# The last 16 rows of five 2 MB loads sent as 8-row transfers, and an encoder's first matmul units reordered around its filter layer

## The reference, cut to what matters

```
xn = rms_norm(x, norm1_w)
q, k, v, r, a_low, hy_in, gates = split(xn @ w_in)            # w_in: 1024 x 8224
o_gla = gla_branch(q, k, v, r, a_low, ...)
h1   = sin(freq * (z @ hy_ffn_w1 + b1))                        # z: 256 x 33, the filter's features
h2   = sin(freq * (h1 @ hy_ffn_w2 + b2));  taps = (h2 @ hy_ffn_w3) * decay
o_hy = hyena_branch(hy_in, ..., taps)
h = x + (sigmoid(g_gla) * (o_gla @ w_branch_gla) + sigmoid(g_hy) * (o_hy @ w_branch_hy)) @ w_out
out = 0
for e in range(32):                                            # 12 MB of weights for each expert
    out += combine[:, e] * (swiglu(hn @ w_gate_up[e] + b) @ w_down[e] + b)
return rms_norm(h + out, norm_f_w)
```

## Time and profile before

| | |
|---|---|
| median of 3 runs | 1237.72 us (1237.39 to 1237.72) |
| the profiled execution's own time | 1237.29 us |
| its span | 1235.4 us |
| PE busy | 1160.8 us, 94% |
| HBM read | 453.29 MB, 368 GB/s over the span |
| granted TensorE clock | 0.999 |

### The profile page before, as it was taken

One profiled execution on the slowest core, in us unless ns is written; L12 is line 12 of the kernel. 1 busy time (PEld: TensorE's weight loads), 2 busy tenths in 40 slices (PEclk: granted clock), 3 DMA queues, 4 the chain that ended last, 5 costly groups with the idle time before them and its releaser, 6 DMA issues.

```text
span 1235.4 us, 13704 instructions
## 1 busy us (share of the span) xinstructions
PE 1160.8 (94%) x5828; PEld 599.6 (49%) x5828; DVE 420.2 (34%) x703; ACT 266.9 (22%) x422; POOL 0.2 (0%) x4
## 2 busy tenths in 40 slices
PE   7999999999999999999999889888988898889987
PEld 6899968888533443443343324333433333333332
DVE  6777878756421221222112112111221121111112
ACT  6866546344210000010010001000100010000002
POOL 0000000000000000000000000000000000000000
PEclk9999999999999999999999999999999999999999
DMA  9454425698999999999999999999999999999996
GB/s 322 147 157 151 148 91 171 217 399 340 365 425 428 427 428 428 427 429 425 429 426 429 428 428 428 427 428 428 427 428 425 429 427 429 427 429 427 427 426 263
DMA packets 67292, 455.25 MB, mean 368 GB/s; under 512 B 6970, under 2 KB 23771, under 8 KB 39966
## 3 DMA queue, kind: packets, MB, share of 16 engines
q1 hardware_dynamic: 65654, 454.06, 89.8%
q10 hardware_dynamic: 1576, 0.29, 0.1%
HBM read 453.29 MB, written 1.05 MB: 368 GB/s over the span
## 4 chain that ended last, share of the span: by engine, by line
PE 64%; DMA 32%; DVE 2%; issue 1%; ACT 1%; DVEq 0%; ACTq 0%
DMA ring<-in_w_gate_up 28%; PE bank L1201 18%; PE bank L1219 12%; PE total L902 6%; PE bank L902 5%; PE total L890 4%; PE bank L890 4%; DMA ring<-in_w_down 3%; PE bank L960 2%; PE bank L1187 2%; PE bank L979 1%; PE total L1233 1%; PE total L1201 1%; PE bank L1208 1%; PE total L950 1%
## 5 line engine op out<-in xcount | busy, mean ns | idle before, releaser
L1201 PE MATMUL bank<-ring,hy_area 128*64 128x512 f32 x1984 | 444.6, 595 | 43.2 <-DMA ring<-in_w_gate_up 43.2
L1201 PEld LDWEIGHTS bank<-ring,hy_area 128*64 128x64 f32 x1984 | 136.8, 137 | 331.4 <-issue 244.6
L1219 PE MATMUL bank<-ring,xn_area 128*64 128x512 f32 x992 | 220.1, 595 | 0.3 <-DMA ring<-in_w_down 0.3
L2119 DVE TENSOR_SCALAR qk_area<-bank 128x512 f32<-128x512 f32 x31 | 21.4, 692 | 361.3 <-PE bank L1201 361.3
L1219 PEld LDWEIGHTS bank<-ring,xn_area 128*64 128x64 f32 x992 | 68.4, 137 | 134.6 <-issue 122.8
L1682 ACT ACTIVATE qk_area<-qk_area 128x512 f32<-128x512 f32 x32 | 20.2, 630 | 456.7 <-DVE qk_area L2119 456.7
L2130 DVE SCALAR_TENSOR_TENSOR xn_area_r<-bank,tmp_area,xn_area_r 128x512 fp32r<-128x512 f32 x31 | 23.3, 751 | 200.5 <-ACT xn_area_r L1693 200.5
L1823 DVE TENSOR_TENSOR front_r<-ring,slot_r 128x1024 fp32r<-128x1024 f32 x60 | 73.1, 1222 | 22.2 <-ACT slot_r L1493 22.2
L1493 ACT CAST slot_r<-ring 128x1024 fp32r<-128x1024 f32 x60 | 62.8, 1049 | 43.5 <-PE bank L902 23.2
L1693 ACT ACTIVATE xn_area_r<-bank,tmp_area 128x512 fp32r<-128x512 f32 x31 | 21.3, 687 | 234.9 <-PE bank L1219 221.0
L979 PE MATMUL bank<-tmp_area_r 128*128 128x512 f32 x124 | 38.0, 426 | 12.8 <-issue 8.6
(11 more groups left out here) (397 smaller groups left out, 1253.2 us busy)
## 6 DMA issues: line engine op xcount, KB each, us to landing
ring<-in_w_gate_up SPq DMA_DIRECT2D x116, 2048.0 KB, 37.0
ring<-in_w_down SPq DMA_DIRECT2D x54, 2048.0 KB, 38.9
ring<-in_w_in SPq DMA_DIRECT2D x31, 1024.0 KB, 5.7
ring<-in_w_gate_up SPq DMA_DIRECT2D x22, 1024.0 KB, 9.4
ring<-in_w_down SPq DMA_DIRECT2D x19, 1024.0 KB, 9.9
ring<-in_w_branch_gla SPq DMA_DIRECT2D x4, 1024.0 KB, 5.2
ring<-in_w_branch_hy SPq DMA_DIRECT2D x4, 1024.0 KB, 7.7
ring<-in_w_out SPq DMA_DIRECT2D x4, 1024.0 KB, 6.3
```

The costliest lines, as they stand in the source:

```text
L1201: last = pe.matmul(to[bk][half * CAP:(half + 1) * CAP, :], xeT[:, j, q, :], where(j, c), start=False, stop=(j == GU_CH - 1), skip_group_ch ...
L1219: last = pe.matmul(banks[to][half * CAP:(half + 1) * CAP, :], half_of(turned, f), where(j, c * D + half * 512), start=(f == 0), stop=(f == ...
L2119: nc.vector.tensor_scalar(gate, made[0][:, :], LIMIT, None, ALU.min).then_inc(gate_ready, 1)
```

## The change

It has two parts.

**In the expert stream**, five of the 170 loads of 2 MB are cut by rows: the first 112 rows in one transfer, and the last 16 in two transfers of 8 rows. They are the 9th of the 2 MB loads and every 34th after it. All other loads stay.

**At the start**, the filter's first matmul moves ahead of the transposes of x (stage `filter_in`), with its wait for `filt_loaded`; DVE's share of the filter layer stays where it was. The function for the first unit becomes `early_unit` and does the first three v units pass by pass; within the first pass it waits for each half of an `xT` tile apart, and ACT signals each half. Chunk 1 is loaded in halves as chunk 0 is, and the rest of `tab` and the small load `w_a` are issued after chunk 1.

```
+EVEN_ROWS = 112
+FEW_ROWS = 8
+SPLIT = tuple(n for n, width in LOADS if width == 2)[8::34]
+
+def row_parts(n):
+    if n not in SPLIT:
+        return [(0, P)]
+    return [(0, EVEN_ROWS)] + [(r, r + FEW_ROWS) for r in range(EVEN_ROWS, P, FEW_ROWS)]
...
-        count[s] += 16
+        count[s] += 16 * len(row_parts(n))
...
-    st = [("xT", n) for n in range(4)] + v0[:1] + [("wa_parts",), ("filter", 1)] + v0[1:] + ...
+    st = [("filter_in",)] + [("xT", n) for n in range(4)] + v0[:1] + [("wa_parts",), ("filter", 1)] + v0[1:] + ...
...
-                if c == 0:
+                if c < 2:
                     for i in range(UNITS_PER_CHUNK):
-                        sp.dma_start(unit_of(i), src[:, 2 * i:2 * i + 2, :]).then_inc([first_loaded, front_loaded[0]][i], 16)
+                        sp.dma_start(unit_of(2 * c + i), src[:, 2 * i:2 * i + 2, :]).then_inc([first_loaded[c], front_loaded[c]][i], 16)
...
-                sp.dma_start(ring[:, s * SLOT:(s + width) * SLOT], rows_of(*CHUNK_ORDER[n], width)).then_inc(moe_loaded[s], 16)
+                src = rows_of(*CHUNK_ORDER[n], width)
+                for r, to in row_parts(n):
+                    sp.dma_start(ring[r:to, s * SLOT:(s + width) * SLOT], src[r:to, :]).then_inc(moe_loaded[s], 16)
...
-            def first_unit():
+            def early_unit(u):
                 a_hi, a_lo = parts_of["xn"]
-                hi, lo = unit_hi(0), unit_of(0, as_r["front"])
-                pe.wait_ge(w_hi_ready, 1)
-                pe.wait_ge(xn_hi_ready, 1)
-                for a in range(TB):
-                    begin(f"v0{a}")
+                hi, lo = unit_hi(u), unit_of(u, as_r["front"])
+                pe.wait_ge(w_hi_ready, u + 1)
+                if u == 0:
+                    for a in range(TB):
+                        begin(f"v0{a}")
                 for m, (act, w) in enumerate(((a_hi, hi), (a_hi, lo), (a_lo, hi))):
                     if m == 1:
-                        pe.wait_ge(w_parts_ready, 1)
+                        pe.wait_ge(w_parts_ready, u + 1)
                     elif m == 2:
-                        emptied(pe, "xT0")
-                    for a in range(TB):
-                        for d in range(2):
-                            last = pe.matmul(bank(f"v0{a}")[:, :], act[:, d, a * P:(a + 1) * P], w[:, d, :],
-                                             start=(m == 0 and d == 0), stop=False)
+                        emptied(pe, f"xT{u}")
+                    for i in range(2):
+                        if m == 0:
+                            pe.wait_ge(xn_hi_ready, 2 * u + i + 1)
+                        for a in range(TB):
+                            last = pe.matmul(bank(f"v0{a}")[:, :], act[:, 2 * u + i, a * P:(a + 1) * P], w[:, i, :],
+                                             start=(u == 0 and m == 0 and i == 0), stop=False)
                 last.then_inc(unit_used, 1)
...
+                elif kind == "filter_in":
+                    pe.wait_ge(filt_loaded, 16 * 4)
+                    pe.matmul(begin("filter1")[0:FFN, 0:SEQ], w1, zfeat, start=True, stop=True).then_inc(fill("filter1"), 1)
...
-                elif stage == UNITS[0]:
-                    first_unit()
+                elif stage in UNITS[:3]:
+                    early_unit(at[2])
```

More of the change, by code:

```diff
@@ L240, in schedule @@
     v0, v1 = tok("v", 0), tok("v", 1)
-    st = [("xT", n) for n in range(4)] + v0[:1] + [("wa_parts",), ("filter", 1)] + v0[1:] + [("a_low",), ("filter", 2), ("abs", 0)]
+    st = [("filter_in",)] + [("xT", n) for n in range(4)] + v0[:1] + [("wa_parts",), ("filter", 1)] + v0[1:] + [("a_low",), ("filter", 2), ("abs", 0)]
     st += v1[:1] + [("gates", 0), ("gates", 1), ("abs", 1)] + v1[1:2] + [("gates", 2), ("gates", 3)]
@@ L315, in tiles_of @@
     if kind in ("abs", "decay", "silu", "softplus", "energy", "energy_rest", "onorm", "gated", "zbias", "Zmul", "parts", "ohy_parts", "bias_parts", "wo"):
+        return []
+    if kind == "filter_in":
+        return ["filter1"]
+    if stage == ("filter", 1):
         return []
@@ L536, in build @@
         rest_loaded = sem("rest_loaded")
-        first_loaded = sem("first_loaded")
+        first_loaded = [sem(f"first_loaded{c}") for c in range(2)]
         filt_loaded = sem("filt_loaded")
@@ L778, in _ @@
                 front(c)
-                if c == 0:
+                if c == 1:
                     sp.dma_start(tab[:, P:], ins["shape_table"][:, P:]).then_inc(rest_loaded, 16)
-                if c == 1:
                     sp.dma_start(w_a.rearrange("p (b n) -> p b n", b=DB),
@@ L1014, in _ @@
                     last.then_inc(fill(f"xT{at[0]}"), 1)
[L1015 to L1024, removed]
+                elif kind == "filter_in":
+                    pe.wait_ge(filt_loaded, 16 * 4)
+                    pe.matmul(begin("filter1")[0:FFN, 0:SEQ], w1, zfeat, start=True, stop=True).then_inc(fill("filter1"), 1)
+                elif stage == ("filter", 2):
+                    pe.wait_ge(sin_ready, 1)
+                    pe.matmul(begin("filter2")[:, 0:SEQ], w2, s1, start=True, stop=True).then_inc(fill("filter2"), 1)
                 elif kind == "proj":
                     project(*at)
-                elif stage == UNITS[0]:
-                    first_unit()
+                elif stage in UNITS[:3]:
+                    early_unit(at[2])
                 elif kind == "tok":
@@ L1488, in _ @@
                     j, = at
-                    s, v = front_arrival(j // UNITS_PER_CHUNK) if j else (first_loaded, 16)
+                    s, v = (first_loaded[j // 2], 16) if j in (0, 2) else front_arrival(j // UNITS_PER_CHUNK)
                     sc.wait_ge(s, v)
@@ L1497, in _ @@
                     for k in range(2):
-                        last = nc.scalar.mul(parts_of["xn"][0][:, 2 * n + k, :], bank(f"xT{n}")[:, k * SEQ:(k + 1) * SEQ], col(C_N1 + 2 * n + k))
-                    last.then_inc(xn_hi_ready, 1)
+                        nc.scalar.mul(parts_of["xn"][0][:, 2 * n + k, :], bank(f"xT{n}")[:, k * SEQ:(k + 1) * SEQ],
+                                      col(C_N1 + 2 * n + k)).then_inc(xn_hi_ready, 1)
                 elif kind == "oT":
@@ L1833, in _ @@
                     n, = at
-                    what, ready, first_col = ("xn", xn_hi_ready, C_N1 + 2 * n) if kind == "xT" else ("ogla", ogla_hi_ready, C_GN)
-                    dve.wait_ge(ready, n + 1)
+                    what, first_col = ("xn", C_N1 + 2 * n) if kind == "xT" else ("ogla", C_GN)
+                    if kind == "xT":
+                        dve.wait_ge(xn_hi_ready, 2 * (n + 1))
+                    else:
+                        dve.wait_ge(ogla_hi_ready, n + 1)
                     hi, lo = parts_of[what]
```

## The result

The changed kernel takes 1302.2 us (median of four runs, 1298.4 to 1308.4), the kernel before 1237.6 in the same session: ratio 1.0527, 95% interval 1.051 to 1.0543, or 64.6 us slower. The forecast was 1257.9, so the direction was right and the size less than a third of the real one. The profiled run is the slowest of the four, 1308.44 us with a span of 1306.7: 71.2 us over the profiled run of before.

What follows compares the result with a forecast made beforehand. PE's own work was taken as the limit until 330 us, the DMA engines from then on. The terms 1.7 (start) and 18.5 (cut loads) on 1237.7 gave 1257.9 us; forecast's own range 1246 to 1272, overall 1235 to 1272.

Steps and rivals of the forecast that it cites:

- The filter's matmul first: Start of PE: waits for the filter's loads until 8.8 us, shifting everything after by +1.7 us (1.2 to 2.1).
- Passes as parts arrive, the second chunk in halves, `tab` and `w_a` later: Start: ACT's 1.49 us wait goes, but off PE's path; later landings delay no first use; worth 0.
- Five cut loads: Expert stream: engines carrying narrow transfers lose 4.9 us per cut load, 24.5 for five, less 6 free: +18.5 us.
- the unknown price: Expert stream: time of one 8-row transfer, between 0.61 and 4.9 us, taken as 2.75.
- 6 us of their loss are free: End of stream: half the engines end about 6 us early; if they carry the narrow transfers, 6 us cost nothing.
- The price by the ports: Expert stream: 8 rows reach two ports, 54 GB/s, 2.4 us a transfer; sum +16.8, about 1254.5 us.
- Rival 1: End of stream: narrow writes aren't slow and the cut evens the engine halves: 1238.9 down to 1236.3 us; chance 0.17.
- Rival 2: Start and end: halves even out and the filter's loads land by 6.9 us, no stall: 1233.7 us; chance 0.14.
- Rival 4: End of stream: the cut has no effect, only the start's 1.7 us counts: 1239.4 us; chance 0.05.
- rival 3: Expert stream: 8-row transfers fall on the late half, nothing is free: 1242.5 us at full speed; chance 0.04.

Runs made afterwards that it cites:

- e1: Kernel before with only the front's edits (filter ahead, passes as parts arrive, second chunk in halves), no load cut: 1239.75 us against 1237.46, ratio 1.0021.
- e9: Changed front without cut loads, the filter's matmul moved back behind the first unit: 1237.36 us against 1237.42 for the kernel before, ratio 0.9998.
- e10: Kernel before, five loads changed, in order: 112 rows alone, 16 alone, 8 + 8 alone, eight transfers of 16 rows 8 apart in two orders: 1259.8 us.
- e11: Kernel before with the five forms of e10 in the reverse order of places: 1264.4 us against 1237.3.
- e2: Kernel before with the five cut loads (112 + 8 + 8 rows) and its old front: 1298.3 us, ratio 1.0509.
- e14: Five cut loads with the old front, each cut load's issue waiting until the load ahead has landed: 1290.5 us, +52.8 on the kernel before.
- e15: Kernel before with the same five waits as e14 but no load cut: 1261.2 us, +23.6.
- e7: Kernel before, five loads issued five ways: consecutive or spaced rows on the written or read side, mixed spaced widths, halves of the columns: 1263.2 us.
- e6: Kernel before, five loads cut five ways: 96 rows plus four 8-row transfers (consecutive, 4 apart), 64 rows 2 apart, 32 consecutive, 32 4 apart: 1271.5 us.
- e13: Kernel before with only the fifth cut load (112 + 8 + 8 rows), run for its profile: 1250.1 us, ratio 1.01.

## Why the prediction was right or wrong

**The filter's matmul first: right.** Forecast 8.8 us for PE's start and 23.84 for `a_low`, measured 8.92 and 24.09; +1.7 forecast, +1.97 in the changed kernel's trace. In e1 it is +2.3, by its trace and by its time, a little over the 2.1 of the bounds. The 0.53 us for the filter's two passes was short: the transposes begin 1.01 us after it. Two small slips change nothing: the tenth slice of the DMA row reads 8, so the engines are full a little later than the ninth, and 48 matmuls at 0.231 us are 11.1 us, not 10.9 (11.0 in the trace, from 13.07 to 24.09).

**Passes as parts arrive, the second chunk in halves, `tab` and `w_a` later: right,** worth 0 (e9, 0.9998).

**Five cut loads: the step that failed.** The bounds of the unknown price were set on the 8-row transfers alone, 0.61 to 4.9 us each, and 2.75 was taken. Two of them by themselves lose 3.3 us (e10, e11), which with their bytes is 1.95 us each, so this term was inside its bounds and too high: 4.9 for a cut in the forecast. The failure lies in the rest of the step, that only the engines with the narrow transfers lose, and that 6 us of their loss are free. What the sum had at nothing was the rest:
- *The 112-row part.* The step compared "two rows where they had one", as if rows 0 to 111 went as fast as they do in a full-width load. Alone they lose 4.9 us at the first place and 10.8 at the last (e10, e11). This term was missing, and it is the largest.
- *All engines lose.* The forecast let only the engines that carry the narrow transfers fall behind, and set 6 us of their lead against it. But the rate of the whole core falls to about half and below (223, 151, 249 GB/s from 410 to 425 us), and from 407.5 to 412.5 no packet keeps its 0.61 us. The stretch is longer than the cut load needs at half rate: 112 rows and two of 8 are 2.1 MB, 4.9 us at 428 GB/s, some 10 at half of it, and a loss of 7.5 to 14.4 us at half rate is a stretch of 15 to 29. There was no lead to spend.
- *The engines' drift.* I read it in the earlier trace rows and counted it as slack. It is the opposite: a cut costs 5.9 us from a start in step, and 7.5 to 14.4 without, the more the further the engines are apart (e2, e14, e15). It also lengthens the end of the stream, which the forecast did not have at all: of e2's 60.8 us, 52.2 are in the five stretches and the rest is in the emptying, where the last load's increments come 18 us apart, 6.8 before.

So the parts measured alone make 2.3 + 60.8 = 63.1 us, against the forecast's 20.2.

**The price by the ports.** The Trainium skill's page "SBUF — State Buffer", section "Door 1: The DMA port swizzle", says that a transfer is bound by how many of 16 ports its partitions reach. On what is written, and not what is read, the runs agree (e7). Worked out by its map: 32 or 64 consecutive rows and 16 rows 8 apart reach 8 ports, and were slow; 32 rows 4 apart and 64 rows 2 apart reach all 16, and were free. On two points the measurements go beyond or against it. Rows 0 to 111 reach all 16 ports by that map and still lose 4.9 us or more. The estimate of 2.4 us for a transfer of 8 rows, worked out from the page's rate per port, gives 4.8 for two, and 3.9 were taken; the sum by it (+16.8) had the same hole as mine. A candidate for the 112 rows starts from the Trainium skill's page "DMA: Bandwidth & Descriptors", section "The descriptor swizzle", by which a 128-partition transfer is split so that each engine writes one port. It gives no such map for other shapes. If they gave each engine consecutive rows, which is a guess, two engines could meet on a port, and the drift would matter because engines ahead and behind would be in differently split loads. That fits packets that take twice their time, the dearer later places and the recovery in e14. But 32 rows 4 apart, where by the same guess two engines share each pair of ports, were free. No run here shows which engine writes which port, so this is argued, not shown.

**The rivals.** Rival 1 needed a price under about 1.2 us for an 8-row transfer, and for two of them alone it was 1.95. Rival 2 needed that too, and the filter's loads by 6.9 us, where they came at 8.92. Rival 4 (no effect) fell at once. Whether the 8-row transfers fall on the early or the late half (rival 3) stays open, and matters little now, since all engines were slowed.

**What stays open:** why 112 consecutive rows are slow and 32 rows 4 apart aren't, and why the engines drift apart in the kernel before. Whether 8 rows 4 apart are cheaper than 8 consecutive ones is open too: e6 compared them at different places, and 1.5 us is about what such readings differ by.

## What to carry over

In this stream a load of all 128 partitions is a form of its own: before cutting one by rows, price every part of it, the wide part first, by one cut load in the running stream and the rate in its window, not the busy share. If a load has to be divided, divide its columns, which cost nothing here. And read engines that finish apart as a danger for whatever disturbs the stream next, not as slack.

## What was not expected of the hardware

- One slow form slows its neighbours: four transfers of 32 consecutive rows (4.9 us of bytes at full rate) lost 16.0 us of the core's stream time at the fourth place, with the share at 1.01 throughout (e6).
- The same 112-row transfer lost 4.9 us at the first of five places, with the engines 2.1 us apart, and 10.8 at the last, with 10.9 (e10, e11).
- Letting the stream run dry costs 3.4 to 3.9 us in the window, and takes 7 to 8 us off the price of a late cut (12.4 to 5.4 at the fourth place, 14.4 to 6.6 at the fifth).
- A starved PE loses clock too: PE is busy for 23.9 of the 35 us of e13's cut, and the granted clock is 0.80 on the mean. In e15 it is 0.50 for some 9 us at the end of the stream, behind a wait of PE of 3 to 4 us.
